# A four-mixer, two-block network on one core: queries scaled in the scores, keys' sums of squares in fp32r two tiles behind, and spectrum products in another place of two seams

## The reference

```
qkv = proj[..., :n_qkv].reshape(bsz, S, 3, N_B_GROUPS, B_HEADS, HEAD_DIM)
for g, (window, dilation) in enumerate(B_PATTERNS):
    q = apply_partial_rotary(rms_norm(qkv[:, :, 0, g], q_gain[g]), cos, sin)
    k = apply_partial_rotary(rms_norm(qkv[:, :, 1, g], k_gain[g]), cos, sin)
    o, lse = dilated_window_attention(q, k, qkv[:, :, 2, g], window // dilation, dilation)
```

## Time and profile before

| | us |
|---|---|
| median of three runs | 3163.09 (3161.67 to 3164.63) |
| the profiled execution | 3160.02 |
| its span, from the first to the last instruction | 3158.3 |
| mean granted PE clock in it | 0.992 of full |
| layer B's column blocks in the trace | about 421 to 970 |
| the two seams | about 2131 to 2157 and 2505 to 2532 |

### The profile page before, as it was taken

The page is one execution under the profiler, slowest core; times in us unless marked ns, Lnnn a source line. Parts: engine busy times, 40 slices in busy tenths (PEclk is TensorE's granted clock), DMA queues, the critical chain, the costliest instruction groups (busy, mean ns, idle before and its releaser), DMA issues.

```text
span 3158.3 us, 38137 instructions
## 1 busy us (share of the span) xinstructions
PE 3097.0 (98%) x15692; PEld 2524.9 (80%) x15692; DVE 1582.0 (50%) x2066; ACT 1100.3 (35%) x1445; POOL 1552.3 (49%) x1138
## 2 busy tenths in 40 slices
PE   8999999999999999999999999899999999999998
PEld 6888878788888888878887888676888787778887
DVE  6654475838473525355466777654211356542113
ACT  3322244444443423332223444434222343242222
POOL 4444475748473555454444422236445556354453
PEclk9999999999999999999999999899999999999999
DMA  5544322222222323355443111112333242223331
GB/s 199 169 156 159 135 83 80 80 67 81 67 81 76 98 94 103 106 185 177 136 160 117 54 41 41 41 54 94 94 106 94 81 147 80 80 67 94 105 95 67
DMA packets 270975, 319.26 MB, mean 101 GB/s; under 512 B 6850, under 2 KB 228689, under 8 KB 270482
## 3 DMA queue, kind: packets, MB, share of 16 engines
q1 hardware_dynamic: 232768, 247.48, 24.2%
q10 hardware_dynamic: 38034, 69.34, 6.5%
HBM read 310.50 MB, written 6.29 MB: 100 GB/s over the span
## 4 chain that ended last, share of the span: by engine, by line
PE 92%; DVE 4%; ACT 1%; issue 1%; POOL 1%; DMA 1%; ACTq 0%; SPq 0%; DVEq 0%
PE ps L558 26%; PE ps L560 25%; PE ps L559 25%; PE psx L803 1%; PE psx L1091 1%; PE ps L1122 1%; PE ps L629 1%; PE psx L782 1%; PE psx L1251 1%; PE ps L597 1%; PE psx L845 1%; POOL Wl L366 1%; PE ps L593 1%; DVE stD L2354 1%; PE ps L594 1%
## 5 line engine op out<-in xcount | busy, mean ns | idle before, releaser
L366 POOL TENSOR_TENSOR Wl<-Wr,Wh 128x512 fp32r<-128x512 f32 x928 | 1271.5, 1402 | 1407.9 <-ACT Wh L1339 1403.8
L558 PE MATMUL ps<-Ah,Wh 128*128 128x512 f32 x1944 | 778.1, 400 | 0.0
L560 PE MATMUL ps<-Ah,Wl 128*128 128x512 f32 x1944 | 757.5, 390 | 0.0
L559 PE MATMUL ps<-Al,Wh 128*128 128x512 f32 x1944 | 757.3, 390 | 0.0
L1339 ACT ACTIVATE Wh<-Wr 128x2048 fp32r<-128x2048 f32 x232 | 443.1, 1910 | 349.6 <-DMA Wr<-in_w_mlp_in_dram 109.6
L558 PEld LDWEIGHTS ps<-Ah,Wh 128*128 128x128 f32 x1944 | 365.1, 188 | 84.8 <-issue 12.0
L559 PEld LDWEIGHTS ps<-Al,Wh 128*128 128x128 f32 x1944 | 365.1, 188 | 81.9 <-issue 8.9
L560 PEld LDWEIGHTS ps<-Ah,Wl 128*128 128x128 f32 x1944 | 364.8, 188 | 77.3
L558 PE MATMUL ps<-Yh,Wh 128*128 128x512 f32 x1088 | 426.0, 392 | 0.1
L559 PE MATMUL ps<-Yl,Wh 128*128 128x512 f32 x1088 | 423.8, 390 | 0.0
L560 PE MATMUL ps<-Yh,Wl 128*128 128x512 f32 x1088 | 423.7, 389 | 0.0
(11 more groups left out here) (408 smaller groups left out, 3893.8 us busy)
## 6 DMA issues: line engine op xcount, KB each, us to landing
Wr<-in_a_w_in_dram SPq DMA_DIRECT2D x48, 1024.0 KB, 6.3
modw<-in_w_mod_dram ACTq DMA_DIRECT2D x96, 512.0 KB, 5.4
Wr<-in_b_w_in_dram SPq DMA_DIRECT2D x40, 1024.0 KB, 5.0
Wr<-in_w_mlp_in_dram SPq DMA_DIRECT2D x32, 1024.0 KB, 5.5
Wr<-in_w_mlp_out_dram SPq DMA_DIRECT2D x32, 1024.0 KB, 5.1
Wr<-in_a_w_out_dram SPq DMA_DIRECT2D x16, 1024.0 KB, 5.1
Wr<-in_c_w_in_dram SPq DMA_DIRECT2D x16, 1024.0 KB, 5.4
Wr<-in_attn_w_qkv_dram SPq DMA_DIRECT2D x12, 1024.0 KB, 5.1
```

The source lines that it names most:

```text
L366: last = pool.tensor_tensor(E.Wl[:, s, part], E.Wr[:, s, part], E.Wh[:, s, part].bitcast(F32), ALU.subtract)
L558: pe.matmul(o, ah, bh, start=first, stop=False)
L559: pe.matmul(o, ah, bl, start=False, stop=False)
L560: return pe.matmul(o, al, bh, start=False, stop=last)
```

## The change

- The sums of squares of a pair of query tiles become eight narrow products (`query_sums`: 32 output rows by 128 tokens each), behind tile 4g+2. ACT takes the root on 256 columns into `rs[:, 1]` (`query_roots`), and behind tile 4g+3 PE transposes it (`columns`), so that it lies with tokens on partitions; DVE takes a small reciprocal (`rate`).
- Queries are no longer scaled: ACT writes them with the gain straight into QB, DVE alone rotates them (`turn_query`, four instructions on 32 partitions), and the norm is multiplied in when the scores are masked: three instructions by column ranges and a maximum in place of one instruction.
- The squares of a key tile are split by ACT and DVE into an fp32r part `rsR` and a rest `sqR` (`square_low`), and PE sums both with two fp32r products (`key_sum`), two tiles behind the tile instead of one. `rsR` and `sqR` lie on the same bytes as `rs` and `sq`. DVE scales a key tile three steps behind the tile (`scaled`, `turn_key`), the last two sooner.
- In both seams `beside(half, 2, 1)` goes behind the last sum of squares and `root_spread` ahead of `beside(half, 3, 0)`; ACT's third pair of copies goes behind the root.
- `ones` is written through an fp32r copy; the mask is loaded over KB instead of QB.

The core of the diff:

```diff
+    E.rsR, = phase(("rsR", [P, 2, S], F32R))
     E.rs = sb("rs", [P, 2, S])
+    E.sqR, = phase(("sqR", [P, 2, S], F32R))
...
-        def ssq(i, t):
-            r = t % 2
-            into(4 + r)
-            pe.wait_ge(*A.of("B", "sq", i, t))
-            pe.matmul(psx[:, r, :], ones[:], sq[:, r, :], start=True, stop=True).then_inc(*X.did("B", "ssq", i, t))
-            emptied[4 + r] = A.of("B", "sqrt", i, t)
+        def key_sum(i, t):
+            b = 5 - t % 2
+            into(b)
+            pe.wait_ge(*V.of("B", "sl", i, t))
+            pe.matmul(bank[b], E.onesR[:], E.rsR[:, t % 2, :], start=True, stop=False)
+            pe.matmul(bank[b], E.onesR[:], E.sqR[:, t % 2, :], start=False, stop=True).then_inc(*X.did("B", "ssq", i, t))
+            emptied[b] = A.of("B", "sqrt", i, t)
+
+        def query_sums(i, g):
+            into(4)
+            pe.wait_ge(*A.of("B", "sq", i, 4 * g + 1))
+            for f in range(2):
+                for q in range(TT):
+                    m = pe.matmul(psx[32 * q:32 * q + 32, 0, f * P:(f + 1) * P], ones[:, 0:32], sq[:, f, q * P:(q + 1) * P], start=True, stop=True)
+            m.then_inc(*X.did("B", "ssq", i, 4 * g))
+            emptied[4] = V.of("B", "rq", i, g)
+
+        def columns(i, g):
+            pe.wait_ge(*A.of("B", "sqrt", i, 4 * g))
+            for f in range(2):
+                m = pe.transpose(psx[:, 0, (2 + f) * P:(3 + f) * P], rs[:, 1, f * P:(f + 1) * P], ident[:])
+            m.then_inc(*X.did("B", "rt", i, g))
...
-            if t:
-                ssq(i, t - 1)
+            if t % 4 == 2:
+                query_sums(i, t // 4)
+            elif t % 4 == 3:
+                if t == 11:
+                    key_sum(i, 10)
+                columns(i, t // 4)
+            elif t >= 4:
+                key_sum(i, t - 2)
...
+                pe.wait_ge(*V.of("B", "turned", i, 8 + hh))
...
-            if k in (4, 5):
-                beside(half, 2, k - 4)
+            if k == 5:
+                beside(half, 2, 0)
+        beside(half, 2, 1)
         emptied[6] = A.of("rsq", {"D": "M0", "M0": "H", "H": "M1"}[L])
 
     def lead(L, half):
         if half is None:
             awake(4)
+        root_spread(L)
         beside(half, 3, 0)
-        root_spread(L)
         beside(half, 3, 1)
...
+        def key_root(i, t):
             act.wait_ge(*X.of("B", "ssq", i, t))
-            if t >= 2:
-                act.wait_ge(*V.of("B", "qk", i, t - 2))
-            act.activation(rs[:, r, :], psx[:, r, :], ACT.Sqrt, bias=eps[:, 0:1], scale=1.0 / P).then_inc(*A.did("B", "sqrt", i, t))
+            act.activation(rs[:, t % 2, :], psx[:, 1 - t % 2, :], ACT.Sqrt, bias=eps[:, 0:1], scale=1.0 / P).then_inc(*A.did("B", "sqrt", i, t))
+
+        def query_roots(i, g):
+            act.wait_ge(*X.of("B", "ssq", i, 4 * g))
+            if g:
+                act.wait_ge(*V.of("B", "qk", i, 4 * g - 1))
+            act.activation(rs[:, 1, 0:2 * P], psx[:, 0, 0:2 * P], ACT.Sqrt, bias=eps[:, 0:1], scale=1.0 / P).then_inc(*A.did("B", "sqrt", i, 4 * g))
...
+            g, f = t // 4, t % 2
             act.wait_ge(*T.of("B", "qk", i, t))
-            if t >= 2:
+            if is_key(t):
+                act.wait_ge(*X.of("B", "ssq", i, 4 * g))
+            elif t >= 4:
                 act.wait_ge(*X.of("B", "ssq", i, t - 2))
             elif i:
                 act.wait_ge(*V.of("B", "y", 0, 2 * (i - 1)))
-            act.activation(sq[:, t % 2, :], ps[t % 3][:], ACT.Square).then_inc(*A.did("B", "sq", i, t))
-            if t >= 3:
-                act.wait_ge(*V.of("B", "qk", i, t - 3))
-            elif i:
-                act.wait_ge(*X.of("B", "pv", i - 1, 0))
-            act.activation(tmp[:, t % 3, :], ps[t % 3][:], ACT.Copy).then_inc(*A.did("B", "cp", i, t))
-            if t % 2 == 0:
-                ahead("B", "qk", i, t // 4, t // 2 % 2)
+            act.activation(sq[:, f, :], ps[t % 3][:], ACT.Square).then_inc(*A.did("B", "sq", i, t))
+            if is_key(t):
+                n = 2 * g + f
+                act.wait_ge(*A.of("B", "sq", i, t))
+                if f:
+                    act.wait_ge(*X.of("B", "rt", i, g))
+                elif t >= 4:
+                    act.wait_ge(*V.of("B", "qk", i, t - 4))
+                act.activation(E.rsR[:, f, :], sq[:, f, :], ACT.Copy).then_inc(*A.did("B", "sh", i, t))
+                if n >= 3:
+                    act.wait_ge(*V.of("B", "qk", i, 4 * ((n - 3) // 2) + 2 + (n - 3) % 2))
+                elif i:
+                    act.wait_ge(*X.of("B", "pv", i - 1, 0))
+                act.activation(tmp[:, n % 3, :], ps[t % 3][:], ACT.Copy).then_inc(*A.did("B", "cp", i, t))
+            else:
+                if i and t == 0:
+                    act.wait_ge(*X.of("B", "s", i - 1, 7))
+                act.activation(E.QB[:, g, f, :], ps[t % 3][:], ACT.Identity, scale=pk(E, "b_q_gain", g)).then_inc(*A.did("B", "cp", i, t))
+            if f == 0:
+                ahead("B", "qk", i, g, t // 2 % 2)
...
+                if t % 4 == 2:
+                    query_roots(i, t // 4)
+                elif t == 11:
+                    key_root(i, 10)
+                elif t >= 4 and t % 4 < 2:
+                    key_root(i, t - 2)
...
+        def square_low(i, t):
+            r = t % 2
+            dve.wait_ge(*A.of("B", "sh", i, t))
+            dve.tensor_tensor(E.sqR[:, r, :], sq[:, r, :], E.rsR[:, r, :].bitcast(F32), ALU.subtract).then_inc(*V.did("B", "sl", i, t))
+
+        def rq(g, f):
+            return stB[:, B_UNITS + 2 * g + f, :]
+
+        def rate(i, g):
+            dve.wait_ge(*X.of("B", "rt", i, g))
+            for f in range(2):
+                dve.reciprocal(rq(g, f), psx[:, 0, (2 + f) * P:(3 + f) * P].rearrange("p (q n) -> p q n", q=TT)[:, :, 0]).then_inc(*V.did("B", "rq", i, g))
...
+        def scaled(i, t):
+            n, r = t // 4 * 2 + t % 2, t % 2
             dve.wait_ge(*A.of("B", "sqrt", i, t))
             dve.reciprocal(rs[:, r, :], rs[:, r, :]).then_inc(*V.did())
             dve.wait_ge(*V.now())
             dve.wait_ge(*A.of("B", "cp", i, t))
-            if i and t == 0:
-                dve.wait_ge(*X.of("B", "s", i - 1, 7))
-            dve.scalar_tensor_tensor(dst, tmp[:, t % 3, :], pk(E, "b_k_gain" if qk else "b_q_gain", g), rs[:, r, :],
+            dve.scalar_tensor_tensor(KB[:, t // 4, t % 2, :], tmp[:, n % 3, :], pk(E, "b_k_gain", t // 4), rs[:, r, :],
...
+        def turn_query(i, t):
+            q, swapped = QB[0:32, t // 4, t % 2, :], PB[0:32, 0, :]
+            dve.wait_ge(*A.of("B", "cp", i, t))
+            if i and t == 0:
+                dve.wait_ge(*X.of("B", "flip", i - 1, 6))
+            dve.wait_ge(*V.now())
+            pinned()
+            dve.stream_shuffle(swapped, q, SWAP).then_inc(*V.did())
+            dve.wait_ge(*V.now())
+            dve.tensor_tensor(swapped, swapped, ropeB[:, 1, :], ALU.mult).then_inc(*V.did())
+            dve.tensor_tensor(q, q, ropeB[:, 0, :], ALU.mult).then_inc(*V.did())
+            dve.wait_ge(*V.now())
+            dve.tensor_tensor(q, q, swapped, ALU.add).then_inc(*V.did("B", "turned", i, t))
...
-            dve.tensor_tensor_reduce(PB[:, u % 2, :], psx[:, u % 2, :], maskB[:, u % 4, :], 1.0, 10 * NEG,
-                                     ALU.add, ALU.max, stB[:, u, 0:1]).then_inc(*V.did("B", "sc", i, u))
+            if u % 4 == 0:
+                dve.wait_ge(*V.of("B", "rq", i, 2))
+            for g, c0, c1 in ((0, 0, 256), (1, 256, 384), (2, 384, 512)):
+                dve.scalar_tensor_tensor(PB[:, u % 2, c0:c1], psx[:, u % 2, c0:c1], rq(g, u // 4)[:, u % 4:u % 4 + 1], maskB[:, u % 4, c0:c1],
+                                         ALU.mult, ALU.add).then_inc(*V.did("B", "sc", i, u))
             dve.wait_ge(*V.of("B", "sc", i, u))
+            dve.tensor_reduce(stB[:, u, 0:1], PB[:, u % 2, :], AX.X, ALU.max).then_inc(*V.did("B", "mx", i, u))
+            dve.wait_ge(*V.of("B", "mx", i, u))
...
+            for t in range(13):
+                if t % 4 == 3:
+                    rate(i, t // 4)
+                if t < 12:
+                    if is_key(t):
+                        square_low(i, t)
+                    else:
+                        turn_query(i, t)
+                k = t - 1 if t > 10 else t - 3
+                if k >= 2 and is_key(k):
+                    scaled(i, k)
+                    turn_key(i, k)
```

More of the change, by code:

```diff
@@ L398, in mixer_b @@
         for i in range(4):
[L399 removed]
             for g in range(3):
[L401 to L407 removed]
+                ahead("B", "qk", i, g, 0)
+                if g:
+                    rope(i, 4 * g - 2)
+                ahead("B", "qk", i, g, 1)
+                if g:
+                    rope(i, 4 * g - 1)
             for g in range(3):
+                if g == 0:
+                    rope(i, 10)
                 ahead("B", "v", i, g)
@@ L906, in mixer_b @@
             value(i, 0)
-            ssq(i, 11)
+            key_sum(i, 11)
             value(i, 1)
```

(9 more changed lines are left out.)

53 lines of the change are left out of this document (22 added, 31 removed).

## The result

| | before | changed |
|---|---|---|
| median | 3163.86 us (4 runs, 3161.67 to 3167.15) | 3211.47 us (4 runs, 3209.14 to 3213.32) |
| profiled execution | 3160.02 us, span 3158.3 | 3209.14 us, span 3207.4 |

The ratio is 1.0152, 95% interval 1.0139 to 1.0165: +47.6 us between the medians, +49.1 between the two profiled executions. The forecast was +27 (3190), with a range up to 3208. The sign and the place were right; the size was off by 20 us.

A forecast was written before the change was run, and what follows sets the result against it. TensorE, busy 3097.0 of 3158.3 us, was taken to bound the kernel. Saving −19.6, root waits +35, clock +9, scores +3.6 and seams −1 gave +27 us: 3190 us, range 3169 to 3208.

The forecast's parts named there:

- Direction and mechanism: Second layer, groups 1 and 2: TensorE waits 4.6 and 4.1 us for query roots in four column blocks, +35 us.
- the steps of the chain: VectorE and ScalarE from the end of tile 4g+1: root ready at 16.6 us, TensorE there at 12.0.
- The clock behind the waits: Behind each of the eight root waits: a clock fall of 1.1 us, +9 us, bounds 0 and 14.
- TensorE's saving: Second layer: key sums −9.6 us and query sums −10.0 us, together −19.6, bounds −18 and −22.
- Scores: Unit 4 of each block: four instructions for mask and maximum take 0.9 us more, +3.6 us, bounds 2.4 and 5.
- Seams: Both seams: wait for squares goes, sixth sum waits, spread comes earlier; −1 us together, bounds −2.4 and +1.
- VectorE in time: Rival, second layer: VectorE is in time and TensorE's saving comes through, 3146 us; chance 0.09.
- Stretched chain: Rival, second layer: VectorE's steps meet POOL, waits of 6 us and full clock falls, +48, 3211 us; chance 0.08.
- The sum: Whole kernel: saving, waits, clock, scores and seams together +27 us, giving 3190 us.

The follow-up runs named there:

- experiment 1: Changed kernel with 16 more fp32r products, read by nobody, ahead of the column transposes of groups 1 and 2: 3194.51 us.
- experiments 1 to 4, 7 and 8: Besides experiment 1 and experiments 2 to 4: the last with changed seams, one product counted to the next stage, 3155.37 us; that with key 10's difference earlier, 3152.58 us.
- experiments 2 to 4: Changed kernel with query roots in the gate's buffer, 3171.77 us; with queries turned later by VectorE, 3181.76; with the root buffer, VectorE's queue reordered, old seams, 3155.16.
- the buffer of its own: Changed kernel with query roots of groups 1 and 2 in the gate's buffer instead of rs[:, 1], VectorE's order kept: 3171.77 us.

## Why the prediction was right and wrong, step by step

- **Direction and mechanism: right.** Eight waits of the transposes for ScalarE's root of 256 columns, that for VectorE's scaling of key 4g−1. 36.9 us measured, +35 on record. The split was off: 5.55 and 3.90 us for g = 1 and 2 in the first block and 5.25 and 3.90 in the others, where I had 4.6 and 4.1. That the sum came so near is in part luck, since the steps of the chain were off both ways. At the first wait they took 15.8 us (447.85 to 463.61) where I had 15.0: the difference 1.77 instead of 0.79, the query's turn 0.4 more, the two scalings 0.75 and 0.82 instead of 1.12 each. VectorE's groups over the loop of the changed kernel:

```profile
L2224 DVE RECIPROCAL rs<-rs 128x512 f32<-128x512 f32 x24 | 80.1, 3337 | 3.4 <-ACT rs L1561 3.4
L2211 DVE TENSOR_TENSOR sqR<-sq,rsR 128x512 fp32r<-128x512 f32 x24 | 32.5, 1353 | 10.1 <-ACT rsR L1586 10.0
L2254 DVE TENSOR_TENSOR QB<-QB,PB 32x512 f32<-32x512 f32 x24 | 32.1, 1336 | 0.8
...
L2227 DVE SCALAR_TENSOR_TENSOR KB<-tmp,PK,rs 128x512 f32<-128x512 f32 x24 | 21.2, 882 | 0.9
```

  The difference takes 1.35 us in the mean and not 0.79, the scaling 0.88 and not 1.12. The query's last addition takes 1.34 in the mean, but 0.68 in the query that heads this chain.
- **The clock behind the waits: the term that failed.** +9 on record, 14 as its bound. What is left of the second layer's +44.3 after 36.9 + 2.6 + 3.4 − 0.5 of waits and −18 of work is **20 us**, 2.5 per wait. The trace says the same directly, with some 39 us of low clock behind the waits of which half is lost, and experiment 1 gets 15.6 us back in the layer. Two errors. I took the 3.40 us of the earlier trace rows as the length of a fall, so 1.7 us as the most that one can cost; here seven of eight stretches are 6.8 us long, and the part that lies behind the wait is 3.9 us in the place shown and up to 6.1 in the others. And I took 1.1 of the 1.7, on the reasoning that part of a fall lies inside the wait, which was so, but of a stretch of twice the length. The rule of the Trainium skill's page "TensorE: Matmul & The Clock Gate", section "HAM oscillation — how this bites in real kernels", that every burst behind a wait starts at the low clock, held for all eight: the trace agrees, and my sum by it, +14, was too low only because of that length. For shorter waits it did not always hold: of the sixteen waits of 1.9 to 3.15 us that the layer has in the kernels of experiments 1 to 4, 7 and 8, five had no low clock behind them.
- **TensorE's saving: nearly.** 19.6 on record, about 18 measured (17.5 to 18.1 in the three kernels of experiments 2 to 4).
- **Scores: right.** +3.6 on record, +3.4 measured, alone and in place.
- **The sum of key 10: missed.** +2.6, four waits of 0.65. I had costed the difference's lateness only for the root's sake, and its own reader, 0.1 us behind the end of tile 11, not at all. These waits hide in part in the others: the root behind them comes when VectorE's queue lets it, so each 0.65 is taken off the wait for it, which would else be 4.55 and not 3.90.
- **Seams: −1 on record, +2.6 measured, sign wrong.** The edit's own part is −1.15 in the first seam, for the reason that I gave, and −1.1 in the second. In the second +1.8 comes from the gate, a wait that I didn't look for, since no data asks for it; it stands as one line, `gate("M0")`, at the head of ScalarE's next stage. The rest is the place of the clock's fall, +1.6 in a seam when it is no longer hidden.
- **Rivals.** "VectorE in time" was put at 3146 and 0.09. As a forecast of this kernel it was rightly low; as a kernel it exists and takes 3153 to 3155. "Stretched chain", 3211 at 0.08, has the measured time by another cause: its longer waits weren't there, its full clock falls were, and more.
- **The sum.** +27 on record and +49.1 between the profiled executions, 22 us short. 11 are the clock, 4.5 the waits for VectorE's chain with those of key 10 (39.5 against 35), 3.6 the seams, 1.6 the saving, and 2.2 lie outside the layer and the seams; the wait of before that went and the scores take off 0.7. The 6 us by which the clock passed its own bound are enough to put the time beyond the range.

Open: what decides whether a wait is followed by the low clock, and for how long. The changed kernel has four waits of the same length, 3.90 us; one has a stretch of 3.4 us and three have 6.8. Of the sixteen waits of 1.9 to 3.15 us, ten had a stretch of 3.4 us, one (3.1 us, with the buffer of its own) had 6.8, and five had none. It was not tried further.

## What to carry to other kernels

When a change gives a buffer a second user, walk the queue of the engine that frees it from the first step that can't be early, and then look for the second reader of the same chain, which shows only when the first wait is gone. Where TensorE waits for some us inside a stream of products, count the wait and then products at 1.2 GHz behind it, here 20 us on 36.9 us of waits of 3.9 to 5.5 us, and less surely behind shorter ones; if the wait can't be taken away, work that nobody reads, put in its place, gave most of that part back here. Before moving a signalled step across a stage's end, look for gates that wait for "all of the stage": they turn an order into a dependence.

## What the runs showed of the chip

- Eight waits of 4.6 us in the mean brought 51.2 us of granted clock 0.5 where there was none; sixteen products of 0.227 us in each wait took it down to 3.4 us in all.
- One fall of the clock costs 0 or 1.6 us in the same code, by whether it lies ahead of a wait or behind it. Differences of 1 to 2 us between two traces of different kernels can be this alone.
- The same addition of 32x512 on VectorE (L2254) takes 1.67 us for query 8 (at 470.13, with the buffer of its own) and 0.68 for query 9 (476.47 above); the products at 473.27 and 474.67 above take 1.47 and 1.76, and the same two take 1.27 and 0.67 at 448.62 and 449.82 in the changed kernel. In the trace with the buffer of its own, GpSimd subtracts weights from 469.47 to 475.89, over the long ones and not over the short one at 476.47. No run here tests whether that is the cause.
